# A three-block model kernel on one core: rotary halves by DMA, two repeating loads for the forget sums, the rounding rest of narrow weights in spare columns, and a channel sum on GpSimd

## The reference, cut to what matters

```python
# first block: low-rank gates, and the layer norm behind the convolution
z = einsum('bler,erk->blek', a_dn.reshape(bsz, L, 2, GLA_RANK), a_up) + a_b   # a_dn: 32 columns of the projection
lg = log_sigmoid(z) / GLA_GATE_NORM
xc = xf - mean(xf, axis=-1)                 # layer_norm over the 1024 channels of hc
# second block, in each of two layers
log_f = log_sigmoid(ff + forget_bias)       # ff: 8 columns, one for each head
cum_f = cumsum(log_f.transpose(0, 2, 1), axis=-1)
t1, t2 = split(t, 2, axis=-1)               # rotary embedding of q_d and k_d, heads of 64
rot = concatenate([-t2, t1], axis=-1)
q_d = t * cos + rot * sin
s_f = einsum('bhqd,bhkd->bhqk', q_f, k_f) * scale + cum_f[q] - cum_f[k]
```

## Time and profile before

| what | value |
|---|---|
| median of three executions | 3516.43 us (3512.21 to 3517.94) |
| the profiled execution | 3512.08 us |
| its span, first to last instruction | 3510.4 us |
| granted TensorE clock, mean | 0.99 |
| PE busy | 3442.5 us, 98% of the span |
| POOL, ACT, DVE busy | 1471.6, 1255.6, 1236.9 us (42%, 36%, 35%) |
| bytes read from HBM | 336 MB |

### The profile page before, as it was taken

How to read it: one execution, slowest core, us unless ns; L and a number is a source line. 1 busy time by engine, 2 the same in 40 slices (tenths; PEclk the granted TensorE clock), 3 DMA queues, 4 the chain that set the end, 5 groups by cost and what they waited for, 6 DMA issues and landing times.

```text
span 3510.4 us, 39172 instructions
## 1 busy us (share of the span) xinstructions
PE 3442.5 (98%) x16124; PEld 2774.4 (79%) x16124; DVE 1236.9 (35%) x2137; ACT 1255.6 (36%) x1924; POOL 1471.6 (42%) x672
## 2 busy tenths in 40 slices
PE   8999999999999999999999999999999999999998
PEld 5777887887888887887777888888887778888776
DVE  3265784533111144212553111111113652111544
ACT  4524323433322332223454222322223553222544
POOL 4222444554544444445423444444445224444332
PEclk9999999999999999999999999999999999999999
DMA  7211223442333323333112223233332122223211
GB/s 269 70 51 55 90 97 111 153 150 73 126 132 120 102 96 132 135 94 108 55 34 96 99 95 95 88 105 98 94 96 88 33 76 95 97 90 102 72 60 55
DMA packets 99294, 341.19 MB, mean 97 GB/s; under 512 B 11371, under 2 KB 11755, under 8 KB 98956
## 3 DMA queue, kind: packets, MB, share of 16 engines
q1 hardware_dynamic: 98352, 336.97, 28.9%
q10 hardware_dynamic: 764, 1.72, 0.1%
HBM read 336.02 MB, written 2.10 MB: 96 GB/s over the span
## 4 chain that ended last, share of the span: by engine, by line
PE 93%; DVE 2%; ACT 2%; DMA 1%; issue 1%; POOL 1%; SPq 0%; DVEq 0%; ACTq 0%
PE ps L1183 26%; PE ps L1185 25%; PE ps L1184 25%; PE ps L1202 2%; PE ps L1204 2%; PE ps L1203 2%; PE ps L1484 2%; PE ps L1511 1%; PE ps L1497 1%; PE ps L1399 1%; PE ps L1269 1%; POOL t L2662 1%; PE ps L1413 0%; PE ps L1239 0%; DMA t<-in_w_ada 0%
## 5 line engine op out<-in xcount | busy, mean ns | idle before, releaser
L2662 POOL TENSOR_TENSOR t<-t,t 128x1024 fp32r<-128x1024 f32 (+2 forms) x588 | 1361.2, 2317 | 1925.3 <-ACT t L1579 1924.3
L1183 PE MATMUL ps<-t,t 128*128 128x512 f32 (+1 forms) x4048 | 1607.7, 397 | 17.4 <-POOL t L2662 8.6
L1185 PE MATMUL ps<-t,t 128*128 128x512 f32 (+1 forms) x4048 | 1583.9, 391 | 0.0
L1184 PE MATMUL ps<-t,t 128*128 128x512 f32 (+1 forms) x4048 | 1579.7, 390 | 0.0
L1183 PEld LDWEIGHTS ps<-t,t 128*128 128x128 f32 x4048 | 764.0, 189 | 184.8 <-issue 17.5
L1185 PEld LDWEIGHTS ps<-t,t 128*128 128x128 f32 x4048 | 763.2, 189 | 167.5
L1184 PEld LDWEIGHTS ps<-t,t 128*128 128x128 f32 x4048 | 764.1, 189 | 157.9 <-issue 1.4
L1579 ACT CAST t<-t 128x1024 fp32r<-128x1024 f32 (+2 forms) x588 | 584.3, 995 | 571.6 <-PE ps L1185 416.3
L2455 DVE TENSOR_TENSOR t<-t,ps 128x512 f32<-128x512 f32 x110 | 75.7, 688 | 531.7 <-PE ps L1185 516.9
L1648 ACT CAST t<-t 128x512 fp32r<-128x512 f32 x158 | 97.0, 621 | 401.4 <-DVE t L2455 361.5
L1835 ACT ACTIVATE t<-t 128x512 f32<-128x512 f32 x88 | 55.6, 632 | 315.1 <-DVE t L2448 315.0
(11 more groups left out here) (285 smaller groups left out, 2283.2 us busy)
## 6 DMA issues: line engine op xcount, KB each, us to landing
t<-in_w_f1i SPq DMA_DIRECT2D x88, 512.0 KB, 3.3
t<-in_w_f2i SPq DMA_DIRECT2D x88, 512.0 KB, 3.3
t<-in_w_ada SPq DMA_DIRECT2D x72, 512.0 KB, 4.4
t<-in_w_ffi SPq DMA_DIRECT2D x44, 512.0 KB, 3.7
t<-in_w_f1o SPq DMA_DIRECT2D x32, 512.0 KB, 3.6
t<-in_w_f2o SPq DMA_DIRECT2D x32, 512.0 KB, 3.5
t<-in_w_gate SPq DMA_DIRECT2D x24, 512.0 KB, 4.0
t<-in_w_out SPq DMA_DIRECT2D x48, 256.0 KB, 2.6
```

Source lines behind the costliest of these rows:

```text
L1183: e.matmul(out, wh[:, at], X.hi[c][:, 0:N], start=c == first, stop=False)
L1184: e.matmul(out, wh[:, at], X.lo[c][:, 0:N], start=False, stop=False)
L1185: m = e.matmul(out, wl[:, at], X.hi[c][:, 0:N], start=False, stop=c == final)
L2662: e.tensor_tensor(k.WL[:, n % NHL, 0:w], k.raw[:, j % NRAW, 0:w], f(k.WH[:, n % NHL, 0:w]), ALU.subtract).then_inc(*k.rest.inc(('rest', j) ...
```

## The change

Four edits. In the diff, `rope` with a minus is PE's and the one with `dma_start` is SP's; the wait for `rot` goes from DVE and from POOL alike.

1. `THIN` names the units `a`, `ff0`, `ff1`. POOL writes their rest not into `WL` but into the padding of `WH`: columns 32 to 63 of each 128. `thin` then issues two matmuls where `products` issues three, high weights and rest by high activations in one and by low activations in the other. The output has the high part's sums in rows 0 to 31 and the rest's in 32 to 63. `gate_in` copies 64 rows, and `AUP` has its rows twice, so the fp32 matmuls behind it have 65 rows and not 33. `forget` scales the two parts apart and adds them.
2. The matrix that turned the halves is gone. SP copies the tile's four blocks of 32 partitions crosswise into a second tile with four DMAs for each rope; the sign is in the sine table. The ring has two buffers.
3. The 16 copies of `CUM` become two DMAs whose source repeats, `cum_loads`, issued behind the `fv` units.
4. POOL adds the eight tiles `CA` into `R[0]` in seven steps between the `sv` units, and PE multiplies the sum once.

```diff
-            for j in range(KT):
-                self.wait_ge('tap', j, 30)
-                m = e.matmul(b, const(k, 'mean'), k.CA[:, j, :], start=j == 0, stop=j == KT - 1)
+            self.wait_ge('conv sum', KT - 1)
+            e.matmul(b, const(k, 'mean'), k.R[0], start=True, stop=True).then_inc(*k.filled.inc(('filled', ('mu',))))
...
+    def conv_sum(self, i):
+        self.wait_ge('tap', i, 30)
+        e.tensor_tensor(k.R[0], k.CA[:, 0, :] if i == 1 else k.R[0], k.CA[:, i, :], ALU.add).then_inc(*k.pool.inc(('conv sum', i)))
...
-    def forget(self, L, R, last):
+    def cum_loads(self, L):
-        for h in range(8):
-            e.dma_start(k.QF[72:80, h, :], k.CUM[0:8, 0, :]).then_inc(*load(k, 'cum').inc(by=16))
-            e.dma_start(k.KF[64:72, h, :], k.CUM[0:8, 1, :]).then_inc(*load(k, 'cum').inc(*([('load', 'cum', L)] if h == 7 else []), by=16))
+        q, kk = (k.CUM[0:8, i:i + 1, :].broadcast_to([8, 8, S]) for i in range(2))
+        e.dma_start(k.QF[72:80, :, :], q).then_inc(*load(k, 'cum').inc(by=16))
+        e.dma_start(k.KF[64:72, :, :], kk).then_inc(*load(k, 'cum').inc(('load', 'cum', L), by=16))
...
+    def rope(self, L, n):
...
+        m = self.take(rope_ring(k, L), 'turn', L, n)
+        self.wait_ge('diff in', L, n)
+        turned = load(k, f'turned {n}')
+        for p in (0, 64):
+            e.dma_start(m[p:p + 32, :], k.DQ[p + 32:p + 64, n, :]).then_inc(*turned.inc(by=16))
+            e.dma_start(m[p + 32:p + 64, :], k.DQ[p:p + 32, n, :]).then_inc(*turned.inc(*([('turned half', L, n)] if p else []), by=16))
...
-    def rope(self, L, n):
...
-        b = self.take(k.banks, 'rot', L, n)
-        e.matmul(b, const(k, 'rot'), k.DQ[:, n, :], start=True, stop=True).then_inc(*k.filled.inc(('filled', ('rot', L, n))))
...
+    def thin(self, out, i, h, X, ks, c0, N, first, final):
...
+        for c in ks:
...
+            e.matmul(out, wh[:, at], X.hi[c][:, 0:N], start=c == first, stop=False)
+            m = e.matmul(out, wh[:, at], X.lo[c][:, 0:N], start=False, stop=c == final)
...
+        e.copy(k.AT[0:64, 0:n], self.bank('a', tag)[0:64, 0:n]).then_inc(*k.act.inc(('gate in', tag), ('free', ('a', tag))))
...
-        e.tensor_tensor(x, self.bank('ff', L)[0:8, :], R.acc[0:8, :], ALU.mult).then_inc(*k.dve.inc(('forget scaled', L), ('free', ('ff', L))))
+        e.tensor_tensor(x, self.bank('ff', L)[0:8, :], R.acc[0:8, :], ALU.mult).then_inc(*k.dve.inc())
+        e.tensor_tensor(y, self.bank('ff', L)[32:40, :], R.acc[32:40, :], ALU.mult).then_inc(*k.dve.inc(('free', ('ff', L))))
+        self.settle()
+        e.tensor_tensor(x, x, y, ALU.add).then_inc(*k.dve.inc(('forget scaled', L)))
...
-        self.wait_ge('filled', ('rot', L, n))
-        e.tensor_tensor(m, self.bank('rot', L, n), k.CS[:, 1, :], ALU.mult).then_inc(*k.dve.inc(('rope sine', L, n), ('free', ('rot', L, n))))
+        self.wait_ge('turned half', L, n)
+        e.tensor_tensor(m, m, k.CS[:, 1, :], ALU.mult).then_inc(*k.dve.inc(('rope sine', L, n)))
...
+                if src[1] in THIN:
+                    raw, wh = (ap.rearrange('p (c m) -> p c m', m=128) for ap in (k.raw[:, j % NRAW, :], k.WH[:, n % NHL, :]))
+                    e.tensor_tensor(wh[:, :, 32:64], raw[:, :, 0:32], f(wh)[:, :, 0:32], ALU.subtract).then_inc(*k.rest.inc(('rest', j), ('read', j)))
```

More of the change, by code:

```diff
@@ L54, in shape_constants @@
     c['causal'] = np.where(t <= s, 0.0, NEG)
[L55 to L60, removed]
     c['hmean'] = same / 64.0
@@ L177 @@
 NRAW, NHL, LOOK, LEAD = (5, 3, 2, 2)
+THIN = ('a', 'ff0', 'ff1')
 def tiles(ap):
@@ L238, in first_memory @@
 def first_memory(k):
-    k.AUP = place(k, 0, [33, 1024])
-    k.AT = place(k, 4, [33, S])
+    k.AUP = place(k, 0, [65, 1024])
+    k.AT = place(k, 4, [65, S])
     k.SIN = place(k, 6, [128, 2, 4, 256])
@@ L1025 @@
     taps = conv_gate = conv_in = head_scale = gla_out = gate = gated = sgu_loads = sgu_in = sgu_norm = sgu_gate = idle
-    conv_norm = spatial = mixture = residual = norm2_gain = ffn_gate = ffn_up = final_tile = idle
-    mix_loads = mix_lambda = forget = diff_in = rope = fox_in = mix_value = idle
+    conv_sum = conv_norm = spatial = mixture = residual = norm2_gain = ffn_gate = ffn_up = final_tile = idle
+    cum_loads = mix_loads = mix_lambda = forget = diff_in = rope = fox_in = mix_value = idle
     scores = weigh = turn = gather = head_out = head_parts = diff_norm = diff_parts = part = scale_parts = final_gain = twin_roots = head = gate_in3 = idle
@@ L1146, in T @@
             i, h = self.unit('split', ('T', name, n, first + s), 128 * len(ks))
-            m = self.products(out, i, h, X, ks, first + s, N, first, first + kt - 1)
+            m = (self.thin if name in THIN else self.products)(out, i, h, X, ks, first + s, N, first, first + kt - 1)
             m.then_inc(*k.filled.inc(('used', h), *([('filled', key)] if s + 8 >= kt else [])))
@@ L1155, in T2 @@
             i, h = self.unit('split', ('T', name, n, 0), 1024)
-            pair.append((key, i, h, self.take(k.banks, *key)))
+            pair.append((key, i, h, self.take(k.banks, *key), self.thin if name in THIN else self.products))
         for c in range(8):
-            for key, i, h, out in pair:
-                m = self.products(out, i, h, X, (c,), 0, S, 0, 7)
+            for key, i, h, out, products in pair:
+                m = products(out, i, h, X, (c,), 0, S, 0, 7)
                 if c == 7:
@@ L1290, in gate_logs @@
             b = self.take(k.banks, 'lg', tag, u, d)
-            m = e.matmul(b, k.AT[0:33, u * 128:u * 128 + 128], k.AUP[0:33, d * 512:d * 512 + 512], start=True, stop=True)
+            m = e.matmul(b, k.AT[0:65, u * 128:u * 128 + 128], k.AUP[0:65, d * 512:d * 512 + 512], start=True, stop=True)
             m.then_inc(*k.filled.inc(('filled', ('lg', tag, u, d))))
@@ L1321, in head_logs @@
                 at = d * 512 + p * 256
-                m = e.matmul(b[:, d * 256:d * 256 + 256], k.AT[0:33, t * 128:t * 128 + 128], k.AUP[0:33, at:at + 256], start=True, stop=True)
+                m = e.matmul(b[:, d * 256:d * 256 + 256], k.AT[0:65, t * 128:t * 128 + 128], k.AUP[0:65, at:at + 256], start=True, stop=True)
             m.then_inc(*k.filled.inc(('filled', ('xl', p, t))))
@@ L2040, in begin @@
         k, e = (self.k, self.e)
-        e.memset(k.AT[32:33, :], 1.0).then_inc(*k.dve.inc(('ones',)))
+        e.memset(k.AT[64:65, :], 1.0).then_inc(*k.dve.inc(('ones',)))
     def low(self, A, t, src, *events):
```

34 lines of the change are left out of this document (24 added, 10 removed).

## The result

The changed kernel took 3498.72 us (median of four, 3493.5 to 3502.41), the kernel before 3516.6 beside it: ratio 0.9956, interval 0.994 to 0.9971, so 15.5 us faster (10.2 to 21.1). Timed again with the experiments it gave 3499.0 against 3511.75, ratio 0.997 (0.9958 to 0.9981), 10.5 us (6.7 to 14.7). The predicted time was 3497.

What follows compares the result with a forecast made beforehand. PE, busy 98%, was taken as the bound. 5.6 + 6.0 + 9.4 - 2.8 - 0.2 (longer loads at the start) + 0.5 = 18.5 us off the median 3516.4 gave 3497.9, stated as 3497; range 3490 to 3507.

Steps and rivals of the forecast that it cites:

- Narrow weights, 5.6: Eight matmuls a unit go: 0.9 us at the context's `a`, 1.1 at the other, 3.6 for two `ff`; together 5.6.
- the first place would give nothing: If 65 rows kept the clock up behind the first eight fp32 matmuls, no gain there: the wait at 101.99 stands behind.
- The mean, 6.0: 14 of the mean's 16 matmuls go, 6.0 us; POOL's seven adds, 9.1 us of new work, are hidden.
- The ropes, 9.4: 32 rotary matmuls give 13.8 us, less 1.7 for hidden rope 0 and 2.7 for the longer forget chain: 9.4.
- The clock behind that wait, -2.8: Third `dv` unit: the wait grows to 3.2 us and the clock falls behind it once in each layer, costing 2.8 us.
- 65 rows, +0.5: Fp32 matmuls with 65 rows, not 33, may keep the clock up: between 0 and 3.4 us, 0.5 taken.
- The copies: Four a rope, 2.9 us to issue and 2.0 to land: halves 4.9 us after `diff_in`; 0.7 us to spare at `dv`.
- PE doesn't see it: In attention DVE waits 0.8 us longer or a little more for the halves, but catches up, so PE isn't delayed.
- 15.3 us to spare over four ropes, 3.8 each: DVE's spare time in attention, busy 31.7 of 47 us, used to find when late halves make the change slower.
- The rival "slower": DVE is held at each sine; gain gone at a landing of 6.2 us and more, 3530 at 8.2; chance 0.05.
- The forget loads, "cost nothing": Two forget loads in place of 16, behind `fv`: PE waits nowhere behind them, so worth nothing and cost nothing.
- late copies (9 to 13): Landing nearer 5.3 us, PE waits for POOL behind ropes 0 and 4: gain 9 to 13 us, 3503 to 3507; chance 0.20.

Runs made afterwards that it cites:

- f_rows65: Kernel before with 65 rows in place of 33 in the gates' fp32 matmuls and the longer AUP, nothing taken away: 3515.21 us, 0.4 us slower.
- a_narrow: Kernel before with the narrow weights alone, with 65 rows and the forget sum's second half added on DVE: 3516.24 against 3513.92 us, 3.9 us slower.
- l_cut8: Changed kernel with each rope's halves moved by 8 copies of 16 rows: 3512.89 us, 1.4 us slower than the kernel before.
- h_cut16: Changed kernel with each rope's halves moved by 16 copies of 8 rows: 3594.34 us, 81.2 us slower than the kernel before.
- j_pool_sine: Changed kernel with the forget step behind the first dv unit and the rope's sine product on POOL, not DVE: 3488.58 us, 21.8 us faster than before.
- e_loads: Kernel before with the forget sums by two late repeating loads and nothing else: 3514.63 against 3513.65 us, 0.7 us slower.
- b_mean: Kernel before with the convolution's tiles added on POOL and one matmul for the mean: 3508.76 us, 5.6 us faster.
- c_ropes_loads: Kernel before with rotary halves by DMA and the two late forget loads, forget chain as it was: 3503.25 us, 10.5 us faster.
- g_forget_later: Changed kernel with the forget step written behind the first dv unit: 3490.67 us, 22.1 us faster than the kernel before.

## Why the prediction was right, point by point

**Bound.** PE had 78 matmul instructions less: 14 of the mean, 32 of the ropes, 32 of the narrow units. The prediction prices them at 6.0 + 13.8 + 6.4 = 26.2 us; the page has 26.8 less, a part of it by the clock, which was low for 70 us in the profiled execution before and for 60 in this one. What moves the time is what waits came back, 8.1 us in the profiled pair. It was right to look for them.

**Narrow weights, 5.6.** No run has the `ff` units alone; their matmuls are gone. At `a` the mechanism was as told, the rest of `v` is waited for at 100.01. But the term kept 1.1 us there with PE at the lower clock ahead of it. With the clock up, PE comes 1.7 us earlier to the same rest, so its wait is 2.38. That is the case the prediction names under the 65 rows, "the first place would give nothing". `f_rows65` bears out the 1.1: there PE comes only the 1.7 us earlier, and waits 0.60.

**The mean, 6.0.** 5.6 measured (2.5 to 8.8), all adds hidden.

**The ropes, 9.4.** Alone with the late loads 10.5 (6.3 to 14.4). Without the forget chain the sum made it 12.1; what it lacked is the wait in attention. The chain's two DVE instructions cost PE 3.05 - 1.67 = 1.38 us a layer, for 1.33 forecast, and the wait that was to be 3.2 us is 3.05.

**The clock behind that wait, -2.8.** This step failed in the changed kernel: no fall in either profile of it, in either layer. `a_narrow` has one behind 2.21 us in the first layer and none behind 2.19 in the second; `l_cut8` has one behind 3.07 in both; `h_cut16` has none behind 3.06 in the first and one behind 3.02 in the second. So the length of this wait doesn't decide it here. What decides isn't settled by these runs.

**65 rows, +0.5.** The falls near 90 and 135 us went, and new ones came at 245, 327 and 378: `f_rows65` shows such a move with nothing else changed (new ones at 270, 328 and 379), at no gain (0.4 slower, within its interval). The fall at 264.56 also went from where it was, but PE then waited 2.87 us for the state's decay at 268.46, not 1.04. Its time is set by ACT's chain whatever the clock is. So the terms of the narrow units and of the rows together were mis-sized: for `a_narrow` they gave a gain of 3.2 us, its matmuls and waits give a loss of 1.1 if the clock is low for as long, 4.3 the other way. The other 2.8 of its 3.9 us aren't in its waits; the low clock of its profile would cover them, but its interval begins at 0.7, and they stay open.

**The copies.** Issue 0.6 each, landing 2.1 by the median and 2.2 to 3.7 at the `dv` and `fv` units beside weight loads: between the bounds and nearer the lower, as chosen. In attention the sine starts 3.9 to 4.0 us behind `diff_in`, not 4.9: the issues are shorter than 0.73, and the 2.0 us to landing count from the start of the last issue and not from its end. No wait for them at the fourth `dv` unit or behind.

**"PE doesn't see it" in attention.** Wrong, by 0.84 us in the first layer and 0.81 in the second. Two steps of it failed. The first is the price: the sine was left at its 0.69 us, but it had one operand in PSUM and now has both in SBUF. Its 16 instances took 0.69 each before and 0.69 to 2.51 after, median 1.57. In 15 of the 16 an instruction of POOL was running when the sine started, and the sine ends 0.55 us behind the end of that one (1704.68 and 1704.13 above). The Trainium skill (SBUF — State Buffer, SBUF: two separate sides) has this rule: a DVE instruction with two SBUF inputs and a GpSimd one that reads SBUF take turns on a port pair, and the later one is blocked for the whole instruction. The trace agrees, 2.50 beside POOL's 2.40, and it agrees the other way round: in `l_cut8` the sine starts 0.05 us ahead of POOL's product and keeps its 0.69, and the product takes 1.77 us where it takes 1.30 alone. `j_pool_sine`, in which the wait is gone, fits this, but it also takes the sine out of DVE's order, so by itself it doesn't tell the slow sine from its place. The second step is the room. "15.3 us to spare over four ropes, 3.8 each" averages over a stretch in which the softmax's maximum stands right behind the sine. In `l_cut8`, with the halves 2.5 us later and the sine quick, PE waits at four of the eight ropes, so the room there was under 2.5 us. The rival "slower" would have decided at a landing of about 4 to 5 us, not 6.2, since `l_cut8` is level with the kernel before (an estimate: 2.0 and 2.5). Its 3530 is also added up wrongly: a gain that is gone at 6.2 and 32 us lost by 8.2 give 3548.

**The forget loads, "cost nothing".** Right for the edit alone (`e_loads`), but "two in place of 16, behind `fv`, are worth nothing by that" misses what they are for in the whole: with the 16 ahead of the copies in SP's order the kernel is 23.2 us slower than before.

**The sum.** 18.5 was forecast, 10.5 and 15.5 were measured. The edits timed alone add up to 12.2 us (-3.9 for `a_narrow`, 5.6 for `b_mean`, 10.5 for `c_ropes_loads`), between the two. By rows: 26.2 - 2.38 (wait at 100) - 0.57 (wait at 144, which `f_rows65` has too) - 1.83 (wait at 268) - 2 x 2.22 (`dv`) - 2 x 0.84 (attention) = 15.3, if the clock is low for as long as before. That is inside the first measurement's interval and 0.6 us beyond the second's. The forecast missed 2 x 0.84 in attention and took the longer waits at 100, 144 and 268 as paid for by the clock. It made up for part of that by 2.8 us of low clock that didn't come. So that the first measurement lies within 2 us of 3497 is in part luck, and the second gain of 10.5 is the one that the prediction gave to late copies (9 to 13), which weren't late.

## What to carry to other kernels

When a matmul is replaced by a copy, reprice the instruction that reads the result: with both operands in SBUF, DVE's product took up to 2.5 us in this kernel when POOL was running ahead of it, and 0.69 otherwise. Room on an in-order engine is what stands between this instruction and the next one that someone waits for, not its idle share over the stretch. An edit that is worth nothing alone may be the one that makes another possible: look at what is behind it in its queue once the other is made. And when two DVE instructions are put into a chain that the rounding of weights stands behind, see whether the rounding can go first: `g_forget_later` took away both waits, 6.1 us, by moving one call.

## What the runs showed of the hardware

- The granted clock's low stretches move with small edits. With 33 rows one begins between 132 and 140 us in all six profiles, and one near 90 in three of them. With 65 rows seven of eight profiles have none between 80 and 240, the eighth one at 103. In their place come ones near 247, 270, 329 and 380: six of the eight 65-row profiles have all four, `f_rows65` three and `a_narrow` two, and a stretch near 250 is there in five of the six 33-row ones too. Behind the `dv` wait of 3.0 to 3.1 us the clock fell in both layers of `l_cut8`, in one of `h_cut16`, and in neither in the two profiles of the changed kernel.
- SBUF to SBUF copies by DMA of 64, 32 and 16 KB take the same 0.6 us to issue on SP; the median landing is 2.1 us for 64 KB and 2.0 for 32 (the view has none for 16). So cutting them from 64 to 32 KB costs issues alone.
- The start, bound by DMA, varies by more than the 0.2 us forecast for the longer `AUP`: the first matmul of `a` starts between 52.9 and 57.0 us with the short one and between 53.4 and 56.4 with the longer one. The 0.2 us can't be told from that.
- A DVE product with both operands in SBUF and a POOL instruction held each other up: 0.69 us alone and up to 2.51 behind a start of POOL's in the changed kernel, and POOL's product 1.77 us, not 1.30, behind a start of DVE's. With one operand in PSUM all 16 took 0.69.
